# Stick-breaking attention with fp32 products on array halves

## The reference, cut to what matters

```python
def stick_breaking_attention(q, k, v):          # q, k, v: 16 heads x 512 x 64
    ...
        z = einsum('bhqd,bhkd->bhqk', qi, k) * 64 ** -0.5
        mask = s_idx[None, :] < t_idx[:, None]
        log_beta = log_sigmoid(z)
        log_one_minus = where(mask, log_sigmoid(-z), 0.0)
        tail = cumsum(log_one_minus, reverse=True) - log_one_minus
        a = where(mask, exp(log_beta + tail), 0.0)
        return einsum('bhqk,bhkd->bhqd', a, v)
# then: o * silu(gate), and x + (that) @ w_out
```

## Time and profile before

| | |
|---|---|
| median of three runs | 1307.05 us |
| profiled execution / its span | 1307.16 / 1305.4 us |
| stick-breaking stage (last q tiles to `out1`) | about 493 to 626.3 us |
| busy over the span: TensorE, VectorE, ScalarE, GpSimd | 98%, 58%, 49%, 26% |
| first scores begin; ScalarE splits the first output weights; head 3's scores end | 501.3; 522.8; 530.7 us |
| granted TensorE clock | 0.999 |
| chain that ended last | TensorE 89%, VectorE 5%, issue 2%, ScalarE 2% |

### The profile page before, as it was taken

The page is one execution under the profiler, slowest core; times in us unless marked ns, Lnnn a source line. Parts: engine busy times, 40 slices in busy tenths (PEclk is TensorE's granted clock), DMA queues, the critical chain, the costliest instruction groups (busy, mean ns, idle before and its releaser), DMA issues.

```text
span 1305.4 us, 17841 instructions
## 1 busy us (share of the span) xinstructions
PE 1285.4 (98%) x6478; PEld 1072.7 (82%) x6478; DVE 751.5 (58%) x1201; ACT 641.7 (49%) x1164; POOL 344.6 (26%) x393
## 2 busy tenths in 40 slices
PE   7999999999999999999999999999999999999998
PEld 6997778788888888888888888888888888888876
DVE  5656889735652235898454653334475434578843
ACT  5379787724532334998244432513343333357632
POOL 2228877400000007774000000000000000479720
PEclk9999999999999999999999999999999999999999
DMA  5232100122222232001223233332223322321111
GB/s 192 82 113 65 45 19 20 49 97 97 97 97 97 97 97 81 17 0 32 97 97 97 80 98 97 97 97 81 79 87 99 120 97 71 122 78 37 50 65 65
DMA packets 70867, 104.66 MB, mean 80 GB/s; under 512 B 3476, under 2 KB 31368, under 8 KB 70664
## 3 DMA queue, kind: packets, MB, share of 16 engines
q1 hardware_dynamic: 69584, 99.44, 24.2%
q0 software_dynamic: 1088, 4.17, 1.0%
q10 hardware_dynamic: 120, 0.05, 0.0%
HBM read 101.55 MB, written 2.10 MB: 79 GB/s over the span
## 4 chain that ended last, share of the span: by engine, by line
PE 89%; DVE 5%; issue 2%; ACT 2%; DMA 1%; SPq 0%; DVEq 0%; POOL 0%; ACTq 0%; POOLq 0%
PE ps L496 24%; PE ps L498 24%; PE ps L497 24%; PE ps L700 3%; PE ps L858 2%; PE ps L713 1%; PE ps L950 1%; PE ps L679 1%; PE ps L1009 1%; PE ps L848 1%; PE ps L727 1%; PE ps L849 1%; DVE sp L2093 1%; PE ps L728 1%; DMA x_tok<-in_x 1%
## 5 line engine op out<-in xcount | busy, mean ns | idle before, releaser
L1696 DVE TENSOR_TENSOR w_lo<-stage,w_hi 128x1024 fp32r<-128x1024 f32 (+4 forms) x188 | 223.9, 1191 | 416.0 <-ACT w_hi L1115 415.7
L1115 ACT ACTIVATE w_hi<-stage 128x1024 fp32r<-128x1024 f32 (+4 forms) x188 | 191.0, 1016 | 457.8 <-PE ps L498 457.1
L496 PE MATMUL ps<-a0h,w_hi 128*128 128x512 f32 x512 | 203.9, 398 | 1.1 <-DVE q_lo L2280 0.8
L498 PE MATMUL ps<-a0h,w_lo 128*128 128x512 f32 x512 | 199.8, 390 | 0.0
L497 PE MATMUL ps<-a0l,w_hi 128*128 128x512 f32 x512 | 199.5, 390 | 0.0
L2381 POOL TENSOR_TENSOR small<-small 128x16 f32<-128x16 f32 (+2 forms) x14 | 32.3, 2312 | 387.9 <-DVE small L1774 284.4
L496 PE MATMUL ps<-w_hi,a0h 128*128 128x512 f32 (+1 forms) x320 | 121.9, 381 | 0.1
L498 PE MATMUL ps<-w_hi,a0l 128*128 128x512 f32 (+1 forms) x320 | 119.9, 375 | 0.0
L497 PE MATMUL ps<-w_lo,a0h 128*128 128x512 f32 (+1 forms) x320 | 119.8, 374 | 0.0
L496 PEld LDWEIGHTS ps<-a0h,w_hi 128*128 128x128 f32 x512 | 96.2, 188 | 20.8 <-DVE w_lo L1696 1.3
L498 PEld LDWEIGHTS ps<-a0h,w_lo 128*128 128x128 f32 x512 | 96.1, 188 | 20.4
(11 more groups left out here) (331 smaller groups left out, 2807.1 us busy)
## 6 DMA issues: line engine op xcount, KB each, us to landing
stage<-in_a_w_in SPq DMA_DIRECT2D x48, 512.0 KB, 3.7
stage<-in_ple_w_gate SPq DMA_DIRECT2D x16, 512.0 KB, 3.3
stage<-in_w_kv_shared SPq DMA_DIRECT2D x16, 512.0 KB, 3.6
stage<-in_sb_w_in SPq DMA_DIRECT2D x16, 512.0 KB, 3.7
stage<-in_a_w_out SPq DMA_DIRECT2D x16, 512.0 KB, 3.4
stage<-in_b_w_in SPq DMA_DIRECT2D x16, 512.0 KB, 3.7
stage<-in_mla_w_in SPq DMA_DIRECT2D x8, 512.0 KB, 3.8
stage<-in_sb_w_out SPq DMA_DIRECT2D x8, 512.0 KB, 3.3
```

Of the source, the lines that this page charges most:

```text
L496: pe.matmul(bank, wh, mh, start=start and not seeded, stop=False, skip_group_check=seeded)
L498: return pe.matmul(bank, wl, mh, start=False, stop=stop, skip_group_check=seeded)
L1115: act.activation(slab(w_hi[r % 2], L, nk, w), slab(stage[r % 4], L, nk, w), ACT.Copy).then_inc(S("hi_ready"), 1)
L1696: dve.tensor_tensor(slab(w_lo[r % 2], L, nk, w), slab(stage[r % 4], L, nk, w), slab(w_hi[r % 2], L, nk, w), ALU.subtract)\
```

## The change

- Scores: one fp32 product per key block with the 64 rows of the head, no split parts. The products alternate between rows 0 to 63 and 64 to 127 of the array. For that, a copy of k and q of the pair with the halves of the partitions exchanged (`k_swap`, `q_swap`) is made by DMAs on the SP queue. Blocks are taken in the order 3, 1, 0, 2, and the masks of blocks 2 and 3 are added by one product. The semaphore for both softplus pieces comes at the end.
- Values: by pair; v is read in place with 64 columns of weights for each head, the two heads into the upper and lower half of one PSUM bank. ScalarE's copy goes. Of `a_T` for even heads there are two buffers, the second in place of the next weights (`a_T2`).
- Order: TensorE does the tails of the even head, values of the pair before, scores of the next even head, tails of the odd head, scores of the next odd head. `tail_done` and `a_done` count by piece.
- `sp_h`, `sp_l` have a buffer for each parity.
- Output: one gate product of 128 partitions per pair on VectorE; both parts on GpSimd (`sb_parts`).
- The loads of p and of the spatial weights on GpSimd's queue wait for the last scores; all loops over pairs are unrolled.

```diff
+            if pair > 1:
+                sp_.wait_ge(S("z_done"), 4 * (pair - 1))
+            for t, to in zip((kT_sh, qT_sb), swapped(pair)):
+                for s in range(2):
+                    sp_.dma_start(to[head_rows(s), :], t[head_rows(s, True), pair, :]).then_inc(S(f"swapped{pair % 2}"), 16)
...
+        def sb_scores(h):
+            pair, s = h // 2, h % 2
+            k_other, q_other = swapped(pair)
...
+            pe.wait_ge(S(f"swapped{pair % 2}"), 64 * (pair // 2 + 1))
+            for n, (j, half) in enumerate(((3, 0), (1, 1), (0, 0), (2, 1))):
                 b, c = KEY_BANK[j]
-                pe.matmul(bank[:, c:c + n], kb[:, kk], qb[:, qq], start=j != 2, stop=False, skip_group_check=True)
-                pe.matmul(bank[:, c:c + n], kb[:, kk], ql[:, qq], start=False, stop=False, skip_group_check=True)
-                t = pe.matmul(bank[:, c:c + P], ident_r[:, :], strict_r[:, :], start=False, stop=False, skip_group_check=True)
+                rows = head_rows(half)
+                k = kT_sh[rows, pair, j * P:(j + 1) * P] if half == s else k_other[rows, j * P:(j + 1) * P]
+                q = qT_sb[rows, pair, j * P:T] if half == s else q_other[rows, j * P:T]
+                if h > 1 and n < 3:
+                    pe.wait_ge(S("a_done"), 3 * (h - 2) + (n + 1))
+                if j == 2:
+                    pe.wait_ge(S("row_done"), h + 1)
+                t = pe.matmul(ps[3 * s + b][:, c:c + T - j * P], k, q, start=j != 2, stop=False, skip_group_check=True)
...
+            pe.matmul(two_blocks(ps[3 * s + 2]), ident_r[:, :], twice(strict_r), start=False, stop=False, skip_group_check=True)
+            for b in (1, 0):
+                pe.matmul(ps[3 * s + b][:, 0:P], ident_r[:, :], strict_r[:, :], start=False, stop=False, skip_group_check=True)\
+                    .then_inc(S("z_done"), 1)
...
+        def sb_values(i):
+            pe.wait_ge(S("a_done"), 3 * (2 * i + 2))
+            if i > 1:
+                pe.wait_ge(S("o2_read"), i - 1)
             for j in range(MB):
-                t = pe.matmul(ps[6 + s][:, j * P:T], v_pair2[:, j, :], a_T[s][:, KEY_COL[j]:KEY_COL[j] + T - j * P],
+                for s in range(2):
+                    c = i * P + s * HD
+                    t = pe.matmul(ps[6 + i % 2][head_rows(s), j * P:T], v_sh[:, j, c:c + HD], attend(i, s, KEY_COL[j], T - j * P),
...
+        for i in range(1, PAIRS):
+            sb_tails(2 * i)
+            sb_values(i - 1)
+            if i < PAIRS - 1:
+                sb_scores(2 * i + 2)
+            sb_tails(2 * i + 1)
+            if i < PAIRS - 1:
+                sb_scores(2 * i + 3)
+        sb_values(PAIRS - 1)
...
+        def weights(h):
+            i, s = h // 2, h % 2
+            if i > 1 - s:
+                act.wait_ge(S("o2_done"), i - 1 + s)
+            for n, (b, c, w) in enumerate(((2, 896, 384), (1, T, 384), (0, 0, T))):
+                act.wait_ge(S("tail_done"), 3 * h + n + 1)
+                act.activation(attend(i, s, c, w), ps[3 * s + b][:, 0:w], ACT.Exp).then_inc(S("a_done"), 1)
...
+        for i in range(PAIRS):
+            weights(2 * i)
...
+            if i < PAIRS - 1:
+                soft(2 * i + 2, 0)
+            weights(2 * i + 1)
+            if i < PAIRS - 1:
+                soft(2 * i + 3, 1)
+        act.wait_ge(S("o2_done"), PAIRS)
...
+        def sb_gated(i):
+            dve.wait_ge(S("o2_done"), i + 1)
+            dve.wait_ge(S("act_lo"), i + first_item["o_sb"])
+            dve.tensor_tensor(tmp[0][:, :], ps[6 + i % 2][:, :], sg[:, i, :], ALU.mult).then_inc(S("o2_read"), 1)
...
+        def sb_parts(i):
+            pool.wait_ge(S("o2_read"), i + 1)
+            pool.tensor_copy(a0h[:, i, :], tmp[0][:, :]).then_inc(S("act_hi"), 1)
+            pool.wait_ge(S("act_hi"), i + (first_item["o_sb"] + 1))
+            pool.tensor_tensor(a0l[:, i, :], tmp[0][:, :], a0h[:, i, :], ALU.subtract).then_inc(S("act_lo"), 1)
```

More of the change, by code:

```diff
@@ L240, in soft_parts @@
     def soft_parts(s, first):
-        return (sp_0[s], sp_h0[s], sp_l0[s]) if first else (sp[s], sp_h, sp_l)
+        return (sp_0[s], sp_h0[s], sp_l0[s]) if first else (sp[s], sp_h[s], sp_l[s])
     a_T = [put("a_T0", [P, TRI], 80), put("a_T1", [P, TRI], 4, of=SGM)]
@@ L427, in slab, with attend @@
         return t[:, 0:nk, 0:w]
+    slot = (lin["out1"].load0 + 1) % 2
+    a_T2 = [nc.alloc_sbuf_tensor_at("a_T20", [P, T], F32, offset=base + 32 * 1024 + 4096 * slot),
+            nc.alloc_sbuf_tensor_at("a_T21", [P, TRI - T], F32, offset=base + 40 * 1024 + 4096 * slot)]
+    def attend(i, s, c, n):
+        if s == 0 and i % 2:
+            return a_T2[0][:, c:c + n] if c < T else a_T2[1][:, c - T:c - T + n]
+        return a_T[s][:, c:c + n]
     loaded = [S(f"loaded{s}") for s in range(4)]
@@ L478, in _ @@
                     load(r)
+                    if r == end_load("sb_q2") - 1:
+                        swap(0)
+                        swap(1)
+                    if r == lin["out1"].load0 + 3:
+                        swap(2)
+                    if r == lin["out1"].load0 + 4:
+                        for pair in range(3, PAIRS):
+                            swap(pair)
                     if r == 3:
@@ L902, in _ @@
         q_tile(1, 0, 4)
-        first_scores(0, KQ0)
+        sb_scores(0)
         q_tile(1, 4, KD)
-        first_scores(1, KQ0)
+        sb_scores(1)
         q_tile(2, 0, KD)
         q_tile(3, 0, 5)
-        sb_tails(0, 0, True)
+        sb_tails(0, True)
         q_tile(3, 5, KD)
-        first_scores(2, KQ1)
-        sb_tails(1, 1, True)
+        sb_scores(2)
+        sb_tails(1, True)
+        sb_scores(3)
         pe.wait_ge(S("sb_q2_read"), 4)
[L913 to L920, removed]
+        for i in range(1, PAIRS):
[7 more added lines that the diff above has]
+        sb_values(PAIRS - 1)
         linear("out1", before=on_the_way())
@@ L1518, in _ @@
         soft(1, 1, first=True)
[L1519 to L1530, removed]
+        for i in range(PAIRS):
+            weights(2 * i)
+            if i == 0:
+                act.wait_ge(S("ring_used"), end_load("sb_q2"))
+                split_to(lin["out1"].load0)
+            if i < PAIRS - 1:
[4 more added lines that the diff above has]
+        act.wait_ge(S("o2_done"), PAIRS)
         rest_of_layer(1, 2, "h_g")
@@ L2126, in _ @@
         split_to(lin["out1"].load0)
-        sb_pair(1, second=True)
-        with dve.Fori(2, PAIRS) as i:
-            link.begin(i, 2, 8)
-            sb_pair(i)
-        link.end(PAIRS - 2)
-        o_lo(PAIRS - 2, a0h, a0l, "o_sb")
-        for s in range(2):
-            o_gate(HEADS - 2 + s, s, PAIRS - 1, ps[6 + s], "o2_done", "o2_read", "o_sb")
-        o_lo(PAIRS - 1, a0h, a0l, "o_sb")
+        for i in range(1, PAIRS):
+            soft(2 * i, 0)
+            soft(2 * i + 1, 1)
+            sb_gated(i - 1)
+        sb_gated(PAIRS - 1)
         def spatial_weights():
@@ L2521, in _ @@
-        kq_parts(1, 1, KQ1)
-        extra_input(1)
-        pool.wait_ge(S("ring_used"), end_load("sb_q2"))
-        no_low(q_low[0], 0)
-        with pool.Fori(2, PAIRS) as i:
-            link.begin(i, 2, 2)
-            for s in range(2):
-                pool.wait_ge(S("z_done"), 4 * i + (2 * s - 2))
-                kq_parts(i, s, KQ)
-        link.end(PAIRS - 2)
-        pool.wait_ge(S("kq_ok"), HEADS)
-        pool.wait_ge(S("q_twice"), HEADS)
+        def sb_parts(i):
[3 more added lines that the diff above has]
+            pool.tensor_tensor(a0l[:, i, :], tmp[0][:, :], a0h[:, i, :], ALU.subtract).then_inc(S("act_lo"), 1)
@@ L2534, in _ @@
+        for i in range(PAIRS - 2):
+            sb_parts(i)
+        pool.wait_ge(S("z_done"), 2 * HEADS)
+        extra_input(1)
         pool.dma_start(ws_tok[:, :, :], ins["a_ws_2"][0].rearrange("g t s -> t g s")).then_inc(S("ws_in"), 16)
-        pool.wait_ge(S("o2_read"), HEADS)
+        for i in range(PAIRS - 2, PAIRS):
+            sb_parts(i)
         pool.wait_ge(S("ws_T"), 4)
```

151 lines of the change are left out of this document (29 added, 122 removed).

## The result

The kernel after takes 1321.02 us (median of 5 runs), the kernel before 1307.06: a ratio on record of 1.0089, 95% interval [1.0065, 1.0112] (the two medians alone give 1.0107). It is slower, by less than 2%, and outside my range of 1301.5 to 1311. The five runs are 1312.2, 1315.1, 1321.0, 1321.3 and 1323.0 us, at mean granted clocks of 0.992, 0.989, 0.985, 0.984 and 0.983: the lower the clock, the longer the run. The profiled execution is the mildest of them, 1312.23 us with a span of 1310.4, so it shows less of the loss than the median has.

What follows compares the result with a forecast made beforehand. The prediction took TensorE to bound the stage, with ScalarE's order setting the pair after the change. Six pair periods (-0.8), end (-0.5) and start (-0.3) gave -1.6 us from 1307.05, so 1305.5 us, range 1301.5 to 1311.

Steps and rivals of the forecast that it cites:

- anything else, such as a granted clock below the present 1.00 with 2 us idle in each pair: Leftover case of the forecast's chances, covering outcomes outside its own case and five rivals; chance 0.04, no time given.
- the 2 us that it saves come back as a wait for ScalarE: TensorE between odd tails and next odd scores: the 2 us saved become idle until ScalarE's weights arrive.
- Pair period 13.6: Loop over head pairs: a pair takes 13.6 us instead of 13.73, set by ScalarE's unchanged order.
- TensorE's work per pair 11.5: TensorE in the pair loop: tails 5.7, values 2.4 and scores 3.44 make 11.5 us, 2 us less than before.
- Values 2.4: Values products of a pair, two heads side by side on column halves: 2.4 us instead of 4.26.
- Scores 1.72: Scores of one head on alternating row halves, masks included: 1.72 us against 1.75, so no gain.
- VectorE "just fits": VectorE's last softplus low half is ready at 7.78 us, before the tails' second part needs it at 7.96.
- Copies at nothing: DMA copies of swapped halves cost nothing; at most 2 us, once, if their cover is gone.
- The sum -1.6: Whole stage: six pair periods -0.8, end -0.5 and start -0.3 us, together -1.6 us.
- 1: Rival: score products on row halves run one after another, pair period 15.2, 1317.5 us; chance 0.08.
- 2, 3 and 4: Rivals: paired products in lockstep, 1309 us, 0.11; VectorE slowed by GpSimd, 1309, 0.08; no switches and free halves, 1301.5, 0.13.
- 5: Rival: only TensorE's work counts, pair period 11.5, 1293 us, needing odd weights ahead of the softplus; chance 0.04.

Runs made afterwards that it cites:

- e9: e5 with a head's weights on ScalarE placed between the two logarithms of the next head's softplus; 1297.26 us, ratio 0.9926.
- e5: e3 with the gate product of a pair one head later in VectorE's queue, no filling products; 1304.88 us, ratio 0.9981.
- e7: e2 with a pair's value products issued head by head instead of by turns; 1315.01 us, ratio 1.0061.
- e6: e2 with each head's four score products all on that head's own row half; 1320.68 us, ratio 1.0103.
- e1: Changed kernel plus six dummy products of 512 columns in each TensorE wait between odd tails and next odd scores; 1303.92 us, ratio 0.9977.
- e2: Changed kernel plus three dummy products of 512 columns in each TensorE wait between odd tails and next odd scores; 1303.89 us, ratio 0.9977.
- e8: e2 without the DMAs that make the swapped copies and the waits for them, output not the reference's; 1303.92 us.
- e3: Changed kernel with value blocks 1 to 3 of a pair moved behind the odd tails and a second odd-weight buffer; 1323.4 us, ratio 1.0127.
- e10: e2 with one filling product instead of three in each wait ahead of odd scores; 1307.35 us, ratio 1.001.

## Why the prediction was wrong

- **The step that failed** is the last case of the chances: "anything else, such as a granted clock below the present 1.00 with 2 us idle in each pair, 0.04", with no time worked out and left out of the range. It is what happened. The term that failed stands in the working ahead of it: "the 2 us that it saves come back as a wait for ScalarE" was priced as if the clock stayed at 1.00 behind that wait. Price: 1321.0 - 1303.9 = 17.1 us at the median, which at 3.0 us a fall would be five or six falls (an estimate; only the run with three was profiled). The forecast was off by 15.5 us, and the clock accounts for all of it. I had written down that a new wait of 2 us would open in each pair of a stage whose clock stood at 1.00 with 0.12 us of idle, and priced the wait as hidden slack. No row of before showed what such a repeated wait does to the clock, so it needed a bound from both sides, as the row halves got; the stage at half clock would have given one. What before does have is two single waits of about 1.2 us, with the clock at 1.00 beside them, and one such gap says little: in after the first four waits of 1.56 us passed as well.
- The Trainium skill, "TensorE: Matmul & The Clock Gate", section A second HAM failure mode: psum-queue depth-cycling, tells of a kernel whose TensorE idles briefly but often between groups of products, and whose clock swings between its two levels for it. The trace agrees: 1.56 us of idle per 13.52, and three stretches at 0.50. That passage spoke against this change, and I did not weigh it.
- **Pair period 13.6: right**, 13.52. Its reason, ScalarE's order, is right too: e9 changes the order, with e5's placing of the values, and gets 12.45. The wait was named in place and releaser (odd scores, ScalarE's weights); 1.56 us against "near 2".
- **TensorE's work per pair 11.5: right.** PE was busy for 11.96, but 0.55 of it are odd scores that wait for ScalarE piece by piece (2.22 us to their tails, 541.37 to 543.59, against 1.67). The parts add up to 2 x 1.67 + 2.30 + 2 x 2.85 = 11.3.
- **Values 2.4: right** (2.30); e7 shows that they depend on the order by turns. **Scores 1.72: right** (1.67); the two halves start 0.01 us apart, and e6 excludes that they only seem to: its pair takes 1.67 us more, near the 2 x 0.85 expected.
- **VectorE "just fits": right.** No wait for it inside the loop; one of 0.9 us at the very end in e1 and e2. Its larger subtraction takes 0.96, as said:

```profile
548.71 0.96 DVE L2089 TENSOR_TENSOR sp_l<-sp,sp_h 128x768 fp32r<-128x768 f32 x1
```

- **Copies at nothing: right** (e8). The first scores came at 501.60, against 501.49 before (the 501.3 of the table is their weight load).
- **The sum -1.6: at full clock -3.1.** Loop 6 x (13.52 - 13.73) = -1.3 (forecast -0.8); end, from head 14's tails to the next stage, 611.49 to 623.88 in e2 = 12.39 against 13.06, -0.7 (-0.5). The next stage starts 2.4 us earlier, so -0.5 is left for the start (-0.3); the last 0.6 lies behind the stage, and I can't place it. Each term came out larger than forecast, all the same way.
- **Rivals.** 1 describes the kernel without the swaps: T = 15.2 worked out, 15.19 measured between e6's odd scores. 2, 3 and 4 are out by the 13.52. 5 named its condition, odd weights ahead of the softplus; e9 puts them ahead of its last part, and the gain is real, but at 12.45 and not 11.5. The rows of the pair shown say where the 1.1 us above 11.3 are: the even scores take 2.11 us up to their tails (558.51 to 560.62), 0.44 more than 1.67, since they follow ScalarE's weights piece by piece; the tails take 3.15 and 3.06 in place of 2.85, as they wait for VectorE's second low half (it ends at 562.30, and the next product begins at 562.36); the values, in two runs between other shapes, take 2.46 in place of 2.30. So TensorE's work is not quite the bound there.

## What to carry to other kernels

When a cut on the bounding TensorE turns into a wait that repeats, price the wait at the lower clock, not at zero: here 1.56 us of idle cost, in some of the pairs, 3 us of slow products behind it, and three products that compute nothing took it back. A cheaper product pays only once the order of the other engines' queues lets it: look for the instruction that frees the bank and what stands ahead of it in its queue. When work moves later, move its readers later in their queues as well (e3 against e5, 18 us).

## What the runs showed of the hardware that I had not expected

- With idle of 1.56 us in each 13.52 the granted clock fell to 0.50 behind three of seven waits in the profiled run, for 6.8 us each time. With 1.3 us (e10) it fell in some runs only, with 0.8 us in none of e2, e7 and e8.
- e6, also with 0.8 us but with its scores one by one on one row half, lost it in all four runs. The idle time alone does not say whether the clock holds.
- The same program varies from run to run by 10 us through this alone (1312 to 1323), where e1, e2, e8 and e9, which keep the clock, vary by about 1 us.
- fp32 products on two row halves of the array overlap (2.13 us of work in 1.28), as those on column halves do (4.26 in 2.30), if they alternate in the queue; in e6 and e7, where they don't, they take 2.35 and 3.93.
